# The last output product of a two-block sequence model, turned to tokens on partitions

## The reference

```python
def rmsnorm(x, w):
    xf = x.astype(jnp.float32)
    y = xf * lax.rsqrt(jnp.mean(xf * xf, axis=-1, keepdims=True) + EPS)
    return (y * w.astype(jnp.float32)).astype(x.dtype)

def stick_breaking_layer(h, norm_w, w_in, w_out):
    ...
    o = jnp.concatenate(outs, axis=1).reshape(bsz, L, SB_WIDTH)
    o = (o * jax.nn.silu(g.astype(jnp.float32))).astype(h.dtype)
    return h + o @ w_out
...
    return rmsnorm(h, final_norm)[:, N_META:].astype(x.dtype)
```

## Time and profile before

| | |
|---|---|
| runs of the kernel, us | 1380.23, 1381.2, 1385.59; median 1381.2 |
| span of the profiled execution | 1381.7 us |
| busy share of the span: TensorE, VectorE, ScalarE, GpSimd | 85%, 45%, 31%, 6% |
| mean granted TensorE clock over the span | 0.940 |
| attention ends, `out4` begins on TensorE | 1339.9 us |
| the last residual tile | 1367.2 us |
| the last copy ends | 1377.3 us |

### The profile page before, as it was taken

One profiled execution on the slowest core, in us unless ns is written; L12 is line 12 of the kernel. 1 busy time (PEld: TensorE's weight loads), 2 busy tenths in 40 slices (PEclk: granted clock), 3 DMA queues, 4 the chain that ended last, 5 costly groups with the idle time before them and its releaser, 6 DMA issues.

```text
span 1381.7 us, 19453 instructions
## 1 busy us (share of the span) xinstructions
PE 1168.3 (85%) x8209; PEld 864.1 (63%) x8209; DVE 625.0 (45%) x1142; ACT 432.9 (31%) x783; POOL 77.9 (6%) x118
## 2 busy tenths in 40 slices
PE   5999979999986656689999665668999999999887
PEld 2777758876832212159994221216999778899766
DVE  3655874555520101146753011015994555545574
ACT  2546523312300000044341000003545663443552
POOL 3000224430000000000000000000000000100000
PEclk9999999999998889899999898989999989999998
DMA  9745964238689999985759999997354213355000
GB/s 330 288 160 206 325 224 139 106 130 307 244 316 409 409 409 409 409 316 183 305 215 377 409 409 410 409 409 284 123 183 140 105 55 129 122 183 184 0 1 31
DMA packets 125099, 338.65 MB, mean 245 GB/s; under 512 B 8657, under 2 KB 11590, under 8 KB 125014
## 3 DMA queue, kind: packets, MB, share of 16 engines
q1 hardware_dynamic: 117536, 334.51, 63.7%
q10 hardware_dynamic: 7478, 2.91, 0.8%
HBM read 336.35 MB, written 1.05 MB: 244 GB/s over the span
## 4 chain that ended last, share of the span: by engine, by line
PE 61%; DMA 26%; DVE 8%; ACT 2%; SPq 2%; issue 1%; ACTq 0%; DVEq 0%
PE bank L684 9%; PE bank L686 9%; PE bank L685 9%; DMA arena<-in_w_up_dram 6%; DMA expert_slots<-in_w_gate_dram 5%; DMA weight_ring<-in_w_up_dram 4%; DMA weight_ring<-in_w_gate_dram 3%; DMA expert_slots<-in_w_down_dram 3%; PE bank L971 3%; PE bank L586 3%; DVE arena L1902 3%; PE bank L1144 2%; PE bank L816 2%; PE bank L663 2%; PE bank L664 2%; DMA weight_ring<-in_ada_w_dram 2%
## 5 line engine op out<-in xcount | busy, mean ns | idle before, releaser
L684 PE MATMUL bank<-input_high,weights_high 128*128 128x256 f32 (+1 forms) x992 | 290.5, 293 | 8.2 <-DVE input_low L1902 7.5
L686 PE MATMUL bank<-input_high,weights_low 128*128 128x256 f32 (+1 forms) x992 | 283.9, 286 | 0.0
L685 PE MATMUL bank<-input_low,weights_high 128*128 128x256 f32 (+1 forms) x992 | 283.8, 286 | 0.0
L1902 DVE TENSOR_TENSOR weights_low<-weight_ring,weights_high 128x1024 fp32r<-128x1024 f32 x142 | 173.6, 1224 | 165.5 <-ACT weights_high L1439 165.2
L684 PEld LDWEIGHTS bank<-input_high,weights_high 128*128 128x128 f32 x992 | 188.3, 190 | 13.7 <-issue 10.6
L1439 ACT ACTIVATE weights_high<-weight_ring 128x1024 fp32r<-128x1024 f32 x142 | 149.6, 1055 | 143.5 <-PE bank L686 143.1
L686 PEld LDWEIGHTS bank<-input_high,weights_low 128*128 128x128 f32 x992 | 188.5, 190 | 0.0
L685 PEld LDWEIGHTS bank<-input_low,weights_high 128*128 128x128 f32 x992 | 187.9, 189 | 0.7
L1902 DVE TENSOR_TENSOR arena<-arena,bank 128x512 f32<-128x512 f32 (+1 forms) x38 | 24.6, 651 | 261.2 <-PE bank L971 240.2
L971 PE MATMUL bank<-arena 128*32 128x512 f32 x384 | 61.2, 773 | 50.0 <-DMA arena<-in_w_up_dram 38.8
L971 PEld LDWEIGHTS bank<-arena 128*32 128x32 f32 x384 | 12.3, 129 | 96.7 <-DMA arena<-in_w_up_dram 43.5
(11 more groups left out here) (414 smaller groups left out, 1748.2 us busy)
## 6 DMA issues: line engine op xcount, KB each, us to landing
weight_ring<-in_ada_w_dram SPq DMA_DIRECT2D x24, 2048.0 KB, 9.4
weight_ring<-in_w_gate_dram SPq DMA_DIRECT2D x16, 2048.0 KB, 23.6
arena<-in_w_up_dram SPq DMA_DIRECT2D x16, 2048.0 KB, 24.2
weight_ring<-in_w_down_dram SPq DMA_DIRECT2D x16, 2048.0 KB, 24.0
arena<-in_w_down_dram SPq DMA_DIRECT2D x12, 2048.0 KB, 20.3
weight_ring<-in_even_w_in_dram SPq DMA_DIRECT2D x9, 2048.0 KB, 8.6
arena<-in_w_gate_dram SPq DMA_DIRECT2D x8, 2048.0 KB, 21.4
weight_ring<-in_w_up_dram SPq DMA_DIRECT2D x8, 2048.0 KB, 16.2
```

The lines of the kernel that those rows point to most:

```text
L684: pe.matmul(b[:, 0:width], hi[:, k, :], XHI[:, k, t0:t0 + width], start=k == 0, stop=False)
L685: pe.matmul(b[:, 0:width], hi[:, k, :], XLO[:, k, t0:t0 + width], start=False, stop=False)
L686: mm = pe.matmul(b[:, 0:width], lo[:, k, :], XHI[:, k, t0:t0 + width], start=False, stop=k == KD - 1)
L1902: return dve.tensor_tensor(out_, a, b, op)
```

## The change

The last product is written the other way round: the tokens' input parts are stationary and 512 columns of the weights move, so that a bank holds 128 tokens by 512 features. Four `VB` banks hold the whole output (two halves of the features, two tiles of tokens). Before the product, TensorE turns the residual into those banks by multiplying each 128 x 128 piece of `XH` with the identity (`residual_rows`: 16 plain float32 matmuls of 128 columns), and the product accumulates onto it. A quarter is now two input tiles by 512 features (`quarter_of`): 2 token tiles x 2 input tiles x 3 passes give 12 matmuls of 512 columns. ScalarE squares each finished bank, with the sum along the row accumulated by the same instruction, and takes logarithm and exponential of one column; VectorE refines it on one column and scales each bank by the row's factor and by the norm's gains, which a new transfer on ScalarE's queue spreads over all partitions (`FNORM`, 512 KB, issued ahead of the attention). The result goes straight to `OUTS`, and SyncE stores each of the four pieces (256 KB) when it is ready. The sums of squares by matmul, the residual adds, the 16 transposes and the four copies go. One row vector less is loaded at the start.

```diff
+            def residual_rows(half, tt, b):
+
+                for k in range(4):
+                    pe.matmul(b[:, k * P:k * P + P], XH[:, 4 * half + k, META + tt * P:META + tt * P + P], ident[:, :],
+                              start=k == 0, stop=False)
+
+            pe.wait_ge(vector_drained, n["v"] - 1)
+            rows = {(half, tt): VB[(n["v"] + 2 * half + tt) % 4] for half in range(2) for tt in range(TT)}
+            for half, tt in list(rows)[0:3]:
+                residual_rows(half, tt, rows[half, tt])
             pe.wait_ge(vector_drained, n["v"])
-            for j in range(2):
-                product(W_OD + 8 + j, 4 * j, T, v_open, v_close, "out4", new_input=j == 0, after=norm_behind(7, T, SQ3))
+            residual_rows(1, 1, rows[1, 1])
+            n["inputs"] += 1
+            for half in range(2):
+                cn = W_OD + 8 + half
+                for m in range(4):
+                    j = len(quarters)
+                    pe.wait_ge(weights_split, j + 1)
+                    hi, lo = (w[:, j % 2].rearrange("p (k a) n -> p k (a n)", k=2) for w in (WHI, WLO))
+                    for tt in range(TT):
+                        b, t = rows[half, tt], slice(tt * P, tt * P + P)
+                        for i in range(2):
+                            k = 2 * m + i
+                            if half == 0 and tt == 0:
+                                pe.wait_ge(input_split, KD * (n["inputs"] - 1) + k + 1)
+                            pe.matmul(b[:, :], XHI[:, k, t], hi[:, i, :], start=False, stop=False)
+                            pe.matmul(b[:, :], XHI[:, k, t], lo[:, i, :], start=False, stop=False)
+                            mm = pe.matmul(b[:, :], XLO[:, k, t], hi[:, i, :], start=False, stop=m == 3 and i == 1)
+                        if m == 3:
+                            v_close(mm, ("final", half, tt))
...
-            for tt in range(TT):
-                for kh in range(2):
-                    b = v_open() if kh == 0 else s_open()
-                    for k in range(4):
-                        pe.wait_ge(h_ready, h_count(7, 4 * kh + k + 1))
-                        mm = pe.transpose(b[:, k * P:k * P + P], h2T[:, 4 * kh + k, tt * P:tt * P + P], ident[:, :])
-                    (v_close if kh == 0 else s_close)(mm, ("final", tt))
...
-            sp.wait_ge(out_copied, 2)
-            sp.wait_ge(scalar_drained, mark["s_end"])
             for tt in range(TT):
-                sp.dma_start(out[0, tt * P:(tt + 1) * P, :], OUTS[:, tt, :]).then_inc(out_done, 16)
-            sp.wait_ge(out_done, 16 * TT)
+                for half in range(2):
+                    sp.wait_ge(out_copied, 2 * tt + half + 1)
+                    c = slice(512 * half, 512 * half + 512)
+                    sp.dma_start(out[0, tt * P:(tt + 1) * P, c], OUTS[:, tt, c]).then_inc(out_done, 16)
+            sp.wait_ge(out_done, 32 * TT)
...
+            act.dma_start(FNORM, final_norm_2.rearrange("(o n) -> o n", o=1).broadcast_to([P, D])).then_inc(final_norm_in, 16)
...
             logs()
-            norm(7, ("out4",), sq=SQ3, nr=NR6)
+            first = len(quarters) - 8
+
+            def final_square(half, tt):
+
+                done = mark[("final", half, tt)]
+                act.wait_ge(vector_filled, done)
+                act.activation(SQF, VB[(done - 1) % 4][:, :], ACT.Square, accum_out=(fsum, ft)[half][:, tt:tt + 1])\
+                    .then_inc(final_squares, 1)
+                act.wait_ge(final_squares, 2 * half + tt + 1)
+
+            while n["high"] < first + 6:
+                high()
             for tt in range(TT):
-                b = take()
-                drained(act.activation(OUTS[:, tt, 512:1024], b[:, :], ACT.Copy))
-            assert n["s"] == mark["s_end"]
+                final_square(0, tt)
+            for _ in range(2):
+                high()
+            act.wait_ge(final_bias, 1)
+            for tt in range(TT):
+                final_square(1, tt)
+                r = frs[:, tt:tt + 1]
+                then(act.activation(r, ft[:, tt:tt + 1], ACT.Ln, bias=fbias[:, tt:tt + 1], scale=1.0 / D))
+                act.activation(r, r, ACT.Exp, scale=-0.5).then_inc(final_seed, 1)
...
-            for m in range(KD):
-                b = take()
-                xm = XH[:, m, META:L2]
-                drained(tt(xm, b[:, 0:T], xm, ADD))
+            for _ in range(KD):
                 split()
...
-            norm(7, "final_norm", 0)
+            dve.wait_ge(final_squares, TT)
+            dve.tensor_scalar(fhalf, fsum, -0.5 / D, -0.5 * EPS, MUL, ADD)
+            dve.tensor_scalar(fbias, fsum, 1.0 / D, EPS, MUL, ADD).then_inc(final_bias, 1)
+            dve.wait_ge(final_bias, 1)
+            dve.wait_ge(final_norm_in, 16)
             for t_ in range(TT):
-                b = take()
-                n["v"] += 1
-                dve.tensor_copy(OUTS[:, t_, 0:512], b[:, :]).then_inc(out_copied, 1)
-            assert n["v"] == mark["v_end"]
+                y, v = frs[:, t_:t_ + 1], fv[:, t_:t_ + 1]
+                dve.wait_ge(final_squares, TT + t_ + 1)
+                then(stt(v, ft[:, t_:t_ + 1], -0.5 / D, fhalf[:, t_:t_ + 1], MUL, ADD))
+                dve.wait_ge(final_seed, t_ + 1)
+                then(stt(v, v, y, y, MUL, MUL))
+                then(stt(y, v, 1.5, y, ADD, MUL))
+                for half in range(2):
+                    c = slice(512 * half, 512 * half + 512)
+                    b = VB[(mark[("final", half, t_)] - 1) % 4]
+                    stt(OUTS[:, t_, c], b[:, :], y, FNORM[:, c], MUL, MUL).then_inc(out_copied, 1)
```

More of the change, by code:

```diff
@@ L53, in vector_rows @@
         (("norm_ffn", 16), ("norm_final", 8), ("dn_conv", 36), ("dn_norm", 1), ("pool_scale", 4),
-         ("sc_conv", 24), ("even_norm", 8), ("odd_norm", 8), ("final_norm", 8), ("ssd_norm", 8)),
+         ("sc_conv", 24), ("even_norm", 8), ("odd_norm", 8), ("ssd_norm", 8)),
         (("lru_conv_w", 32), ("lru_conv_b", 8), ("lru_b_a", 8), ("lru_b_x", 8), ("lru_lambda", 8),
@@ L347, in build @@
         IDB = A[:, 23012:23012 + P // 2].bitcast(BF16)
-        OUTS = at(2176, 2, 1024)
+        OUTS, FNORM, SQF = at(2176, 2, 1024), at(0, 1024), at(1024, 512)
+        fsum, fbias, fhalf, frs, fv, ft = (at(1536 + 4 * i, 2) for i in range(6))
         vec_src = {"c": c.rearrange("a (r p) -> (a r) p", p=P), "c_ctx": c_ctx.rearrange("(r p) -> r p", p=P),
@@ L359, in build @@
                    "odd_norm": odd_norm_2.rearrange("o (r p) -> (o r) p", p=P),
-                   "final_norm": final_norm_2.rearrange("(r p) -> r p", p=P),
                    "ssd_norm": ssd_norm_2.rearrange("o (r p) -> (o r) p", p=P),
@@ L421, in build @@
         out_copied, out_done = sem("out_copied"), sem("out_done")
+        final_norm_in, final_squares, final_bias = sem("final_norm_in"), sem("final_squares"), sem("final_bias_ready")
+        final_seed = sem("final_rstd_seed")
         def cols(w, c0, n=512):
@@ L486, in chunk, with quarter_of @@
             return slot(n).rearrange("p (k w) -> p k w", k=k)
+        def quarter_of(j):
+            cn, m = quarters[j][0:2]
+            if cn >= W_OD + 8:
+                return chunk(cn)[:, 2 * m:2 * m + 2, :].rearrange("p k (a n) -> p (k a) n", a=4)
+            return chunk(cn)[:, :, m * P:m * P + P]
         def h_count(i, k=KD):
@@ L1235, in _ @@
-            mark["v_end"], mark["s_end"] = n["v"], n["s"]
+            def residual_rows(half, tt, b):
[6 more added lines that the diff above has]
+                residual_rows(half, tt, rows[half, tt])
@@ new lines, in _ @@
+            pe.wait_ge(vector_drained, n["v"])
+            residual_rows(1, 1, rows[1, 1])
[17 more added lines that the diff above has]
+                            v_close(mm, ("final", half, tt))
+                    if m < 3:
+                        mm.then_inc(weights_used, 1)
+                        n["used"] += 1
+                    quarters.append((cn, m) + ((weights_used, n["used"]) if m < 3 else (vector_filled, n["v"])))
+                released[cn] = (weights_split, len(quarters))
@@ L1433, in high @@
                     return
-                cn, m, _, _ = quarters[j]
+                cn, m = quarters[j][0:2]
                 if m == 0 or j == 0:
@@ L1438, in high @@
                     act.wait_ge(quarters[j - 2][2], quarters[j - 2][3])
-                act.activation(WHI[:, j % 2], chunk(cn)[:, :, m * P:m * P + P], ACT.Copy).then_inc(weights_high, 1)
+                act.activation(WHI[:, j % 2], quarter_of(j), ACT.Copy).then_inc(weights_high, 1)
                 n["high"] += 1
@@ L1915, in split @@
                     return
-                cn, m, _, _ = quarters[j]
                 dve.wait_ge(weights_high, j + 1)
-                w = chunk(cn)[:, :, m * P:m * P + P]
-                tt(WLO[:, j % 2], w, WHI[:, j % 2].bitcast(F32), SUB).then_inc(weights_split, 1)
+                tt(WLO[:, j % 2], quarter_of(j), WHI[:, j % 2].bitcast(F32), SUB).then_inc(weights_split, 1)
```

(17 more changed lines are left out.)

## The result

Over 12 executions each on the same chips, the kernel before took 1387.32 us (median; 1378.90 to 1390.59) and the changed one 1377.47 us (1369.08 to 1383.40). The ratio is 0.9933 with a 95% interval of 0.9911 to 0.9955: the change makes the kernel 0.7% faster, some 9 us. The forecast was 1369.9 us with a range up to 1375.0 and a gain of 11.3 us. The direction held, and the gain predicted from the profile lies inside the interval (1 - 11.3/1387.3 = 0.9919); the time itself lies outside the range. All ratios here leave out a slow run, one over 1.5% above the fastest of its kernel, of which there was a single one, 1385.12 us among the six runs of the kernel with both further edits.

What follows compares the result with a forecast made beforehand. It took TensorE's last product as the bound, then a serial tail and store. Gains of 3.3 (product), 6.1 (to last copy) and 1.9 (store) made 11.3 us, so 1381.2 - 11.3 = 1369.9 us, range 1366.8 to 1375.

Steps and rivals of the forecast that it cites:

- The start: Before the last product: residual matmuls take 3.9 us, the gap hides 2.4, and they delay the product by 1.5 us.
- The clock: At the last product's start: residual matmuls fill TensorE's 2.3 us idle, so the clock doesn't fall: -1.7 us, bounds 0 and -1.7.
- The product: Last product: quarters of 12 matmuls take 2.79 us, 22.3 against 22.7 in all (-0.4); seven norm sums go (-3.0).
- The tail: After TensorE's end: VectorE's small steps and scalings bound it, ending 4.25 us behind TensorE, 9.35 us earlier than before.
- The store: Output store at the end: 2.4 us behind the last piece instead of 4.33, with 1.92 hidden.
- The sum: Span 1381.7 to 1370.4, 11.3 us less: 3.3 in the product, 6.1 up to the last copy, 1.9 in the store.
- the prediction's four terms: TensorE's end in the last product: +1.5 start, -1.7 clock, -0.4 product, -3.0 norm sums, adding to -3.6 us; it used 3.3.
- Costed at nothing: Gains transfer ahead of the attention, half 0 squares, bias columns with their waits, and the vector loaded at the start: no cost.
- the base: Whole kernel's time before the change: 1381.2 us, taking the profiled span of 1381.7 as 0.5 above the runs' median.
- the rivals: Clock falls or preparation sets the pace (0.17), tail worth less (0.08), half clock in the product (0.02), nothing beyond noise (0.08).
- the noise rival: Whole kernel: the change does nothing beyond noise, including shifts in the first 1337 us; time 1374 to 1382, chance 0.08.
- the signs of being wrong: Clock 0.5 after 1340, TensorE idle before quarters, VectorE idle between token tiles' scalings, or attention beginning later than 1301.9.

Runs made afterwards that it cites:

- both further edits: Changed kernel with 6 of the residual's 16 matmuls moved into gaps before the last two `stick_out` groups, and scalings shared by VectorE and ScalarE: 31.29 us last stretch, ratio 0.9886.
- Sharing the tail: Changed kernel, with VectorE multiplying half 0 by the gains early and ScalarE scaling it at the end, VectorE scaling half 1 alone: last stretch 32.55 us.
- kernel before with its gap filled: Kernel before, with five dummy matmuls of 272 columns after the last `stick_out` group, where TensorE waits for the first low part: last stretch 43.29 us.
- the residual in part earlier: Changed kernel with 6 of the residual's 16 matmuls moved ahead of the last two `stick_out` groups, into TensorE's 0.68 us waits: last stretch 31.80 us.

## Why the prediction was right, and where it was wrong

**The start.** Forecast +1.5, measured +1.17: the residual's matmuls take (1352.49 - 1348.90) / 16 = 0.224 us each, not 0.245. The hiding is shown by moving them behind the gap, which costs 4.0 us, 2.4 of it for the wait and 1.6 for the clock.

**The clock.** Forecast -1.7 with the clock kept up. It stayed at 1.00; filled with something else, the same gap gave the kernel before 1.5, and the gap left open cost the changed kernel 1.5 to 1.6. So the mechanism is shown from both sides, and the size is 1.5 to 1.6: the prediction had rounded 3.7 / 18 = 0.206 us up to 0.21 and then took 0.095 for the difference to 0.118, where 0.088 was right.

**The product.** Forecast 22.3, measured 22.4 us; the matmuls follow at 0.233 us, as in the first product. The norm sums are gone and the weights' preparation never held TensorE. The estimate by the 216 ns that the prediction took from the Trainium skill ("TensorE: Matmul & The Clock Gate", Back-to-back issue gap) would have been 1.6 us too low. That section calls the 216 ns the gap of an isolated matmul and gives about 131 ns for a long stream of weight loads and matmuls, which is what runs here; this trace, with its 233 ns for the float32r form, agrees with neither.

**The tail.** Forecast 4.25 us from TensorE's end to the last scaling, bound by VectorE; measured 4.04, with the two scalings at 0.70 each and not 0.72, and less between the small steps. Sharing the tail moved its end by 1.2 us, so VectorE was the bound.

**The store.** Forecast 2.4 and 1.9 hidden. Measured 2.5 from the last scaling's end to the end of the span, and 2.1 lost when nothing is hidden. The prediction's estimate by the Trainium skill ("DMA: Bandwidth & Descriptors", Anatomy of one DMA), 2.6 us, is as near, but the section is about transfers that GpSimd issues; here SyncE issues them.

**The sum.** 11.3 forecast, 11.7 measured in the last stretch, in two profiles of each kernel. By parts, all counted from the start of the last group of `stick_out`: TensorE ends 3.6 us earlier (forecast 3.3, though the prediction's four terms make 3.6), 6.3 are won from there to the last copy or scaling (6.1), and 1.9 in the store (1.9). The sum isn't right by errors that cancel.

**Costed at nothing.** The transfer's issue takes 0.35 us on ScalarE's queue and delays neither the table load nor the scores, as shown above. The vector no longer loaded at the start shows no effect either: ScalarE's third table load comes at 122.7 to 123.7 us in the three profiles of the kernel before or with its gap filled, and at 122.9 to 124.6 in the other nine.

**What failed is the base.** The step that failed is "the profiled span stands 0.5 above the median of the runs, so the time is 1381.2 - 11.3". The three runs that it took as the kernel's time happened to lie low: 12, with these three among them, gave a median of 1387.32, and 19 others 1389.19, from 1378.9 to 1395.1. Of the 43 times of this kernel in these two sets and the comparison with itself, 1381.2 is the fifth lowest. That draw was bad luck; that the range had no room for it was not. Of the 7.6 us between forecast and result, 1387.3 - 1381.2 = 6.1 are this, and 1.4 are the gain, which came out at 9.9 between the medians. A second slip lies in the same sentence: it sets a span beside run times. A run's time is about 2 us more than its span (1383.40 for the span of 1381.4 after), so the profiled execution of before was one of about 1383.7, 2.5 above the median used and not 0.5. The range allowed 2.5 us of spread downward and only as much upward as the rivals took; the noise rival had 0.08 and a time of 1374 to 1382, in which the result lies and which a plain shift of the base reaches. Of the signs of being wrong that it named, one came, the attention beginning later than 1301.9 (1310.96 after), but it came in the kernel before too (1304.01 in its second profile), so it was no sign of the change.

**Where the spread lies.** It is in work that no version touches. The attention begins anywhere from 1295.7 to 1306.4 us, in the kernels before from 1297.3 to 1303.0, and takes 38.4 to 41.2. Two stretches take one of two lengths each, in either kernel: the attention 38.7 us in two profiles and 40.8 to 41.2 in nine (the last section shows the clock in both), and the stretch that took 35.53 us in the first profile of before 35.5 to 35.6 in eight of the twelve profiles and 37.8 to 37.9 in four. It took 37.82 in the kernel before with its gap filled, whose program is the same up to there, at a clock of 0.87 and not 0.94:

```profile
942.33:980.15 37.82, 35.12 (x177) 30.21 (x170) 24.27 (x58) 14.91 (x30) 2.80 (x4) 0.87 0.52 181
```

That the granted clock makes the difference there is read from the rows. By a change it is shown only where gaps were filled: ahead of the product, in several profiles, and ahead of the attention, in a single one.

**What stays open.** Both ratios of the changed kernel (0.9933 and 0.9928) lie a little above the 0.9916 that 11.7 us make. The intervals hold 0.9916, so no loss upstream is shown; one of 1 to 2 us is not excluded either. With the repeated runs put together, 43 of the kernel before average 1387.5 us and 20 of the changed one 1377.1, which are 10.4 apart, give or take some 2.3. I didn't try the new transfer and the missing vector by themselves, because their comparison would tell 3 us at best; the profiles show no loss at the two places where they act.

## What to carry to other kernels

Sum a local edit by a stretch between two instructions of the profile, and take the kernel's level from as many runs as there are: here the stretch repeated to 0.04 us and the whole by 15, so a good sum on a base of three runs missed the range. Work that has to be done anyway is best placed where TensorE would otherwise wait: here it was free as far as it fitted the wait, and it kept the granted clock up, which even dummies did, for 1.5 us. When a tail is shortened, look at what was hidden behind it: sharing the scalings brought 1.2 us on the engines and 0.5 at the end, because the store's bytes became the bound.

## What the runs showed of the hardware that I had not expected

The clock fell in nearly the same place and came back at two different times. Ahead of the attention TensorE idles for 1.3 and 1.8 us. In the profile before, the clock then stays at the half level for 3.4 us, worked out from the first two of these lines (a stretch of t us at a mean clock of c has 2 x (1 - c) x t at the half level):

```profile
1302.00:1303.00 1.00, 1.00 (x8) 0.78 0.00 0
1303.00:1306.00 3.00, 2.90 (x14) 0.51 0.00 0
1306.00:1311.00 5.00, 3.68 (x32) 1.00 0.00 0
```

In the profile after it stays there for 10.2 us, from about 1310.5 to 1320.8, though TensorE was busy for 4.5 of 5 and 3.1 of 4 us:

```profile
1310.00:1311.00 1.00, 0.04 (x2) 0.77 0.00 0
1311.00:1316.00 5.00, 4.49 (x20) 0.50 0.00 0
1316.00:1320.00 4.00, 3.10 (x16) 0.50 0.00 0
1320.00:1325.00 5.00, 5.00 (x40) 0.92 0.00 0
```

The eleven profiles without the fillings all have one of these two lengths: 3.4 us in the first profile of before and in the kernel with the residual in part earlier, which has the new transfer too, and 10.2 in the other nine, among them the second profile of before. The attention takes 38.7 us with the short one, 40.8 to 41.2 with the long one and 38.4 with none. So neither length belongs to a kernel; which one an execution gets was not found out.

The four stores of 256 KB, whose rows are half as long, moved about 380 GB/s when they ran back to back (382 from 1379 to 1381 us of the kernel with all stores last), where the two of 512 KB moved about 405 (403 from 1378.5 to 1380.5 us before); that is some 0.2 us on a store of 1 MB.
